# Two output projections: seven of eight head tiles of their first two units computed during the last head

## The reference

```
block 1: x = x + gated_deltanet(rms_norm(x)) ; x = x + squared_relu_mlp(rms_norm(x)) ; x = rms_norm(x)
  gated_deltanet: 8 heads of 128; o[head] = chunked delta rule(q, k, v, beta, g), normed, * silu(z)
                  return o.reshape(B, S, 1024) @ w_out          # "dn_out", 1024 x 1024
block 2: x = x + mx[2] * (concat([att_x, hg_x]) @ w_out)         # "w_out", 1024 x 1024
  att_x: attention, 8 heads of 64 (512 columns)
  hg_x : gated linear attention in both directions, 4 heads of 128 (512 columns), normed, * silu(g)
         x = x + mx[5] * swiglu(modulate(rmsnorm(x))) ; x = rmsnorm(x)
```

## Time and profile before

| | us |
|---|---|
| median of 3 runs | 3566.88 |
| profiled execution, its own time | 3562.82 |
| its span | 3560.8 |
| PE busy | 3268.4 (92%) |
| DVE busy | 1518.3 (43%) |
| ACT busy | 990.6 (28%) |
| POOL busy | 470.3 (13%) |

### The profile page before, as it was taken

One profiled execution on the slowest core, in us unless ns is written; L12 is line 12 of the kernel. 1 busy time (PEld: TensorE's weight loads), 2 busy tenths in 40 slices (PEclk: granted clock), 3 DMA queues, 4 the chain that ended last, 5 costly groups with the idle time before them and its releaser, 6 DMA issues. The chain is left out here.

```text
span 3560.8 us, 37721 instructions
## 1 busy us (share of the span) xinstructions
PE 3268.4 (92%) x15995; PEld 2652.8 (75%) x15995; DVE 1518.3 (43%) x1721; ACT 990.6 (28%) x1279; POOL 470.3 (13%) x335
## 2 busy tenths in 40 slices
PE   7899899997989999999868999998967899999998
PEld 5778787776768888888755666877856688888886
DVE  3454545444256444333354764544453322212224
ACT  4444444443221111111332333222312211111111
POOL 1333232232100000000110000321331000000001
PEclk9999999998999999999988999999978999999999
DMA  3111111011313332111210001000003111111111
GB/s 114 36 42 42 36 36 42 13 42 48 112 65 107 118 118 91 46 48 48 89 49 24 9 9 31 30 30 30 13 24 136 36 48 48 48 48 48 48 45 57
DMA packets 77816, 187.18 MB, mean 53 GB/s; under 512 B 7121, under 2 KB 29009, under 8 KB 77649
## 3 DMA queue, kind: packets, MB, share of 16 engines
q1 hardware_dynamic: 77648, 184.77, 15.8%
HBM read 165.15 MB, written 16.84 MB: 51 GB/s over the span
## 5 line engine op out<-in xcount | busy, mean ns | idle before, releaser
L472 PE MATMUL ps<-b 128*128 128x512 f32 x5952 | 1495.6, 403 | 51.1 <-DVE b L1172 22.0
L472 PEld LDWEIGHTS ps<-b 128*128 128x128 f32 x5952 | 1105.5, 191 | 295.1 <-DVE b L461 17.2
L1281 PE MATMUL ps<-b 128*128 128x512 f32 x2592 | 607.5, 395 | 0.5 <-DVE b L1412 0.5
L1281 PEld LDWEIGHTS ps<-b 128*128 128x128 f32 x2592 | 485.7, 188 | 117.6 <-DVE b L1412 1.0
L461 DVE TENSOR_TENSOR b<-b 128x1024 fp32r<-128x1024 f32 (+1 forms) x206 | 279.2, 1358 | 380.6 <-ACT b L453 374.0
L2537 PE MATMUL ps<-b 128*128 128x512 f32 (+1 forms) x1584 | 365.5, 388 | 36.2 <-DVE b L1635 14.4
L453 ACT ACTIVATE b<-b 128x1024 fp32r<-128x1024 f32 (+1 forms) x206 | 214.6, 1045 | 560.6 <-PE ps L1281 463.3
L2537 PEld LDWEIGHTS ps<-b 128*128 128x128 f32 x1584 | 285.3, 198 | 95.9 <-issue 41.7
L1141 POOL TENSOR_TENSOR b<-b 128x1024 f32<-128x1024 f32 x24 | 58.9, 2452 | 1740.9 <-ACT b L1147 1740.4
L1026 POOL TENSOR_TENSOR b<-b 128x512 f32<-128x512 f32 x112 | 148.0, 1337 | 507.6 <-DVE b L930 396.9
L1327 ACT ACTIVATE b<-ps 128x1024 f32<-128x1024 f32 x54 | 55.4, 1026 | 401.3 <-PE ps L472 401.3
(11 more groups left out here) (271 smaller groups left out, 3414.5 us busy)
## 6 DMA issues: line engine op xcount, KB each, us to landing
b<-in_down SPq DMA_DIRECT2D x52, 512.0 KB, 3.7
b<-in_mod SPq DMA_DIRECT2D x96, 256.0 KB, 2.6
b<-in_gu SPq DMA_DIRECT2D x44, 512.0 KB, 3.6
b<-scratch SPq DMA_DIRECT2D x40, 512.0 KB, 4.9
b<-in_dn_in SPq DMA_DIRECT2D x32, 512.0 KB, 4.8
b<-in_up SPq DMA_DIRECT2D x32, 512.0 KB, 3.8
b<-in_win SPq DMA_DIRECT2D x26, 512.0 KB, 4.0
scratch<-b SPq DMA_DIRECT2D x20, 512.0 KB, 3.3
```

What stands on the lines that cost most here:

```text
L472: ins = e.matmul(ps[:, c], w, h[:, k, c], start=first and k == 0 and i == 0, stop=last and k == KT - 1 and i == 2)
L1281: ins = e.matmul(ps[:, c], w, u[:, at[k], c], start=k == 0 and p == 0, stop=k == n - 1 and p == 2)
```

## The change

1. High and low parts of all activations get one home. `b_hi` and `b_lo` (8 tiles each) stay allocated for the whole kernel and replace the delta rule's `d_hi`/`d_lo`, the projections' `phi`/`plo`, the MLPs' `hi`/`lo` and the 1024 token columns of block 2's `hi`/`lo`; the 256 context columns get `c_hi`/`c_lo`.
2. During the last head of each mixer the side work goes on with units 0 and 1 of the output projection, over head tiles 0 to 6. Tiles come from DRAM into three buffers of the mixer that are free by then, are split by ACT and DVE into `b_hi`/`b_lo`, and are handed out as 28 steps (7 tiles x 2 parts x 2 units, 84 matmuls). The split of unit 2's weights goes with the first step.
3. How many steps each call hands out in the last head changes: in head 7 of block 1 one per step in turns 3 and 4, one per level (after the first half's first product), one per chunk of the serial loop, then 6 before and 3 after the second half's transposes; in head 3 of block 2 half of what each call named before (37 in all, of which the first 16 are the gate).
4. The last head's own tile (tile 7) is no longer stored and loaded back. Its gating in block 2 is done in two halves (in block 1 it was already), and each half is split from the buffer it lies in. PE then does tile 7 of units 0 and 1 by halves, then unit 2 alone over all tiles, then units 3 to 7 as before.
5. The residual is loaded after the last split of tile 7, all eight tiles in a row.

```
+def mix_steps(on):
+    on.mix_tile(0)
+    for k in range(KT - 1):
+        if k + 1 < KT - 1:
+            on.mix_tile(k + 1)
+        for part in range(2):
+            for i in range(2):
+                on.mix_piece(i, k, part)
+                yield None
...
     def delta_halves(self, side, h, halves):
+        turn = 0
         while halves:
-            for g in list(halves):
+            for f, g in enumerate(list(halves)):
                 step = next(g, self)
                 if step is self:
                     halves.remove(g)
-                else:
+                elif h < H1 - 1:
                     side.fill(1 if step is None else step)
+                elif turn < 5 or (step == 2 and f == 0):
+                    side.fill(1)
+            turn += 1
+            side.mixing = h == H1 - 1 and turn >= 3
...
+    def sp_mix(self, e, sig, name, free):
+        for k in range(KT - 1):
+            for sem in free(k):
+                e.wait_ge(*sem)
+            if k >= 3:
+                e.wait_ge(*sig[2].at("pl", k - 3))
+            e.dma_start(self.heads[name][0][k % 3], self.scratch[0][:, k, :]).then_inc(*self.pol[k % 3].up(name, k))
+
+    def pe_mix(self, e, sig, name, i, k, part):
+        j = UNIT[name, 0] + i
+        if k == 0 and part == 0:
+            e.wait_ge(*self.ww.at(j))
+        if i == 0 and part == 0:
+            e.wait_ge(*sig[2].at("pl", k))
+        self.gemm_piece(e, self.psl[i], j, k, part, self.b_hi, self.b_lo)
+
+    def act_mix(self, e, sig, name, k):
+        j0 = UNIT[name, 0]
+        if k == 0:
+            self.act_weights(e, j0 + 3)
+            e.wait_ge(*self.gm.at(j0 - 1))
+        e.wait_ge(*self.pol[k % 3].at(name, k))
+        e.activation(self.b_hi[:, k, :], self.heads[name][0][k % 3], ACT.Copy).then_inc(*sig[1].up("ph", k))
+
+    def dve_mix(self, e, sig, name, k):
+        if k == 0:
+            self.dve_weights(e, UNIT[name, 0] + 3)
+        e.wait_ge(*sig[1].at("ph", k))
+        e.tensor_tensor(self.b_lo[:, k, :], self.heads[name][0][k % 3], self.b_hi[:, k, :].bitcast(F32),
+                        ALU.subtract).then_inc(*sig[2].up("pl", k))
+    # act_mix_last, dve_mix_last: the same for one half (512 columns) of tile 7, from the gated output itself
...
+    def gla_fill(self, h, n):
+        return n if h < 3 else n // 2
...
     def pe_project(...):
+        for half in range(2):
+            c = slice(512 * half, 512 * half + 512)
+            e.wait_ge(*V.at("pl", KT - 1, half))
+            for i in range(2):
+                a, b = blk(self.whi[(j0 + i) % SPL], KT - 1), blk(self.wlo[(j0 + i) % SPL], KT - 1)
+                for w, h in ((a, self.b_hi), (a, self.b_lo), (b, self.b_hi)):
+                    ins = e.matmul(self.psl[i][:, c], w, h[:, KT - 1, c], start=False, stop=w is b)
+                if half:
+                    ins.then_inc(*self.gm.up(j0 + i))
+        for i in range(2, KT):
+            e.wait_ge(*self.ww.at(j0 + i))
+            e.wait_ge(*(free if i == 2 else V.at("add", i - 3)))
+            for k in range(KT):
+                for part in range(2):
+                    ins = self.gemm_piece(e, self.psl[i % 3], j0 + i, k, part, self.b_hi, self.b_lo)
+            ins.then_inc(*self.gm.up(j0 + i))
...
     # sp_project: wait for pl(7, second half), load the eight residual tiles, then the weights of the later units
```

More of the change, by code:

```diff
@@ L174, in projections @@
                 yield from self.project(h, which)
+        while not self.mixing:
+            yield "idle"
+        yield from mix_steps(self.on)
     def fill(self, n=1):
@@ L276, in gla_projections @@
         side.ready.add((h, "g"))
+    yield from mix_steps(side.on)
 def piece_steps(k, part, ctx):
@@ L780, in act_delta @@
         side.finish()
+        for f in range(2):
+            self.act_mix_last(e, self.mm1, "dn_out", f, V.at("of", H1 - 1, f))
         for s in self.dn:
@@ L903, in dve_delta @@
         side.finish()
+        for f in range(2):
+            self.dve_mix_last(e, self.mm1, "dn_out", f)
         for s in self.dn:
@@ new lines, in dve_mix_last, with sp_project @@
+    def dve_mix_last(self, e, sig, name, half):
+        c = slice(512 * half, 512 * half + 512)
+        e.wait_ge(*sig[1].at("ph", KT - 1, half))
+        e.tensor_tensor(self.b_lo[:, KT - 1, c], self.heads[name][1][:, c], self.b_hi[:, KT - 1, c].bitcast(F32),
+                        ALU.subtract).then_inc(*sig[2].up("pl", KT - 1, half))
+    def sp_project(self, e, m, sig, name, xsrc):
+        j0 = UNIT[name, 0]
+        e.wait_ge(*sig[2].at("pl", KT - 1, 1))
+        for i in range(KT):
+            e.dma_start(m["x"][:, i, :], xsrc[:, i, :]).then_inc(*self.xl[i].up(name))
@@ L2154, in act_gla @@
         side.finish()
-        self.act_weights(e, UNIT["w_out", 0] + 3)
+        for f in range(2):
+            self.act_mix_last(e, self.mm2, "w_out", f, V.at("of", 3, f))
         self.after_gla(e)
@@ L2410, in __init__, with mix_tile, mix_piece @@
         self.k, self.e = k, e
+    def mix_tile(self, k):
+        pass
+    def mix_piece(self, i, k, part):
+        if k == 0 and part == 0:
+            self.e.wait_ge(*self.k.dn[1].at("ev", 4 * H1 - 2 + i))
+        self.k.pe_mix(self.e, self.k.mm1, "dn_out", i, k, part)
     def unit(self, j):
@@ L2522, in __init__, with mix_tile, mix_piece @@
         self.bank = [k.ps[:, 0:512], k.ps[:, 512:1024], k.ps[:, 1024:1024 + TC]]
+    def mix_tile(self, k):
+        pass
+    def mix_piece(self, i, k, part):
+        if k == 0 and part == 0:
+            for p in ((0, 1), (2,))[i]:
+                self.e.wait_ge(*self.sig[1].at(*self.free[p]))
+        self.k.pe_mix(self.e, self.k.mm2, "w_out", i, k, part)
     def unit(self, u):
@@ L2536, in piece @@
                 e.wait_ge(*self.sig[1].at(*self.free[p]))
[L2537 to L2538 removed]
+            x = (s.c_lo if i == 1 else s.c_hi)[:, k, :] if p == 2 else blk4(s.b_lo if i == 1 else s.b_hi, k, p)
+            ins = e.matmul(self.bank[p], (hi, hi, lo)[i], x, start=k == 0 and i == 0, stop=last)
             if last:
```

225 lines of the change are left out of this document (103 added, 122 removed).

## The result

The changed kernel takes **3485.44 us** (median of 4 runs, 3484.33 to 3487.43), the kernel before beside it 3567.35 (3566.58 to 3573.31): a ratio of 0.9767, 95% interval 0.9751 to 0.9784. On a second chip it came to 0.9784 (0.9769 to 0.9799). The forecast was 3513, its range 3500 to 3534: right in its sign, 28 us too small in its gain, and outside the range. In the profiled executions the span went from 3560.8 to 3482.4, 78.4 us.

What follows compares the result with a forecast made beforehand. TensorE, busy 92% of the span, was taken as the bound, with time to gain at the ends of the two mixers. Gains of 19.7 + 33.6 = 53.3 us gave a median of 3513 us, range 3500 to 3534.

Steps and rivals of the forecast that it cites:

- D: Block 1, head 7: what the 84 matmuls put into its chain cost, 14.6 us, from 6.5 to 28.
- the first level: Head 7, turn 3: starts near 835.5 instead of 827.16; with 1.6 us got back, it costs 6.8 us.
- the end of the levels: Head 7: the levels' six steps, 20 matmuls at full price, add 4.9 us, from 1 to 9.8.
- the chunk loop and the end: Head 7: side matmuls and splits in the chunk loop cost 2.0 us, six steps before L711 0.9.
- The wait of turn 3: Head 7: TensorE waits for tile 0's low part behind VectorE's work, idle about 8 us.
- S: Block 2, head 3: net price of the side work, 3.2 - 3.5 + 0.6 = 0.3 us, from -4 to +7.
- from level 5 to level 6: Head 3: waiting for tile 0's low part, level 6 starts near 8.4 us instead of 5.5; value 3.2 us.
- that gain: Head 3 after level 6 starts: side matmuls raise TensorE's clock, bringing 3.5 us, from none to 5.5.
- Both gaps: TensorE's 6.27 us (block 1) and 6.40 us (block 2) gaps in the projections would go without successor.
- The sum for the handed-out work: Both blocks together: 19.7 us gained in block 1 and 33.6 in block 2, 53.3 us.
- One home for the parts adds no instruction.: Shared activation parts: no added instruction; a possible wait dismissed because writers come after earlier readers; no time counted.
- the rivals: Everything hides, 3501 us (0.17); joins cost more, 3534 (0.11); slower, 3617 (0.03); only the gaps go, 3541 (0.02).

Runs made afterwards that it cites:

- e7: Changed kernel with only TensorE's products in head 7 put off from the third to the fifth turn: 3486.70 us, ratio 0.9773.
- e4: Changed kernel with all 28 handed-out steps run only after each last head's own work, none beside it: 3514.28 us, ratio 0.9846.
- e1: Changed kernel with only the address of the parts moved by 640 bytes, off a multiple of 4096 from the weights: 3507.25 us, ratio 0.9827.
- e2: Kernel before with only its weight buffers moved by 640 bytes, no side work handed out: 3525.55 us, ratio 0.9884.
- e3: Changed kernel with every big moving operand a multiple of 4096 bytes behind the weights: 3472.01 us, ratio 0.9727.
- e5: Changed kernel with the hand-out of head 7 begun after turn 5 instead of the third, on all engines: 3480.90 us, ratio 0.9758.

## Why the prediction was wrong

**What held.**
- Head 7's price D was forecast at 14.6 us. From head 6's store to the last gating's end it went from 64.98 us (814.68 to 879.66) to 79.12 (817.15 to 896.27): 14.1. By its parts: the first level starts 9.2 us later against the store (838.81 - 817.15 = 21.66, before 827.16 - 814.68 = 12.48), forecast 8.3; at the end of the levels it is 11.8 (forecast 6.8 + 4.9 = 11.7), and the chunk loop and the end add 2.3 (forecast 2.9). The wait of turn 3 came where it was said to come, and e7 bears out that it costs: the head is 5.0 us shorter without it, of which 2.4 are left once the twelve products stand behind the head.
- Head 3's price S was forecast at 0.3 us. From head 3's start (the store of head 2) to the rows' end it is 88.0 us in both kernels, and 90.7 in the second profile of the changed one. The wait cost more than foretold: from level 5 to level 6 it is 9.75 us (forecast 8.4, before 5.5). From level 6 to the rows' end it went from 40.0 to 35.9. But the forecast had that gain come of the projection's products there, and in e4, which has none of them in head 3, the same stretch takes 36.2 (2609.79 to 2645.97) and the whole head 83.1 (from 2562.92). So the sum came out by luck in part: most of that gain comes without those products, and the products themselves cost head 3 some 5 us.
- Both gaps went, and none came in their place before the stream's end.
- The sum for the handed-out work: with the parts 640 bytes off, as most of them were before (the delta rule's lay on a multiple), the change is worth 3560.8 - 3505.3 = 55.5 us in the profiles (e1), against a forecast of 53.3. In the medians on that chip it is 61.1; the profiled execution of the kernel before was a quick one, 3562.82 against 3568.32. Up to the ends of the two projections e1 gains 20.4 and 36.3 us, where 19.7 and 33.6 were forecast. On the aligned pair, e2 to e3, it is 3525.55 - 3472.01 = 53.5 us, of which some 6 come of the first MLP's last 64 bytes.

**The step that failed**: "One home for the parts adds no instruction." That is true, and it was priced at nothing because only instructions and waits were counted. One home also changed the distance of the MLPs' and projections' operands from the weights. From e1 to the changed kernel, which differ in nothing but that, it is 3505.3 - 3482.4 = **22.9 us** in the profiles and 21.8 in the medians: by the table 7.2 + 3.1 + 7.8 in the MLPs less 1.1 at the first one's beginning, and 2.5 and 3.5 in the stretches that hold the projections and the input projections. 55.5 + 22.9 are the 78.4 us. None of the rivals had it, and the range took its bounds from D and S alone. e1, the change without the new distance, lies inside the range at 3507.25.

**A term that was mis-sized**: the 288 matmuls of units 2 to 7 were priced at 11.7 + 58.75 = 70.5 us and 12.0 + 57.51 = 69.5. They took 65.45 and 65.30. The price of the 240 was taken from rows that begin after a 6 us gap, while the forecast itself said that the gap goes. Behind the gap of block 1 the first 14 matmuls took 6.08 us, at a granted clock of 0.51:

```profile
930.58:936.66 6.08, 6.08 (x14) 4.79 (x15) 4.40 (x2) 0.13 (x1) 3.11 (x1) 0.51 0.65 192
```

In e1 the two streams take 67.36 and 66.94 us. So in the second one 2.6 us of the 4.2 are the missing restart and 1.6 the address, in the first 3.1 and 1.9.

**How the address works is not shown.** The runs show that the pitch of these products, each with a weight load of its own, depends on the distance of the moving operand from the weights, repeating every 256 bytes. The Trainium skill (page "TensorE: Matmul & The Clock Gate", section "Step-by-step: what each phase is for") gives TensorE two independent SBUF read ports, one for the moving operand and one for the weights, and a pitch of about 216 ns for 512 columns at full clock. By that the addresses would not matter; in these runs they do, and the measurement decides. Nor does the pitch come to 216 here: the lowest mean of a long stream is 226.7 ns. Whether the same holds without a weight load per matmul, or at distances that are no multiple of 64 bytes, was not tried.

## What to carry to other kernels

An edit that moves a buffer can change the speed of instructions that it leaves alone: list the addresses of both operands of the busiest product before and after, and price them as a term with bounds. A pitch that differs between two stages with the same instruction at the same clock is the sign of it. The rows of before had only a faint one (44.61 us for 192 products in the second MLP, which is 232.3 ns each, and 233.3 in the first), because none of their long streams ran at the fast distance. When a gap goes, take the price of what follows it from a stream in full run, not from the stream behind the gap. When a total moves, look whether the stage that the edit touches moved: e5 gained by the clock of another stage. And when an experiment moves a step, move it on one engine at a time, or the partner's work moves along and the wait comes again.

## What the runs showed of the hardware

A matmul of 512 columns in fp32r, in a stream in which each has its own weight load, starts every 226.7 ns when the moving operand lies a whole multiple of 256 bytes of the partition from the weights, 228.9 ns at 64 bytes, and 232.3 to 233.3 at 128 and 192. In short groups between small matmuls it hardly shows: neighbours start 264.7 ns apart on average at a multiple of 256 and 265.3 at 128 past one. Moving 640 bytes of other data to the front of the memory made the kernel before 1.2% faster with no instruction changed (ratio 0.9884, 0.9867 to 0.9900).
